# A hybrid decoder layer on one core: normal form in two fused operations, transposes and logits between the halves of the output projection, and routing of the first six tiles ahead of the last

## The reference

```python
def layer_norm(x, g, b):
    mu = jnp.mean(x, axis=-1, keepdims=True)
    var = jnp.mean(jnp.square(x - mu), axis=-1, keepdims=True)
    return (x - mu) * lax.rsqrt(var + LN_EPS) * g + b

mix = jnp.concatenate([y_conv, y_sb, y_gla], axis=-1) @ w_out
x = layer_norm(ALPHA * x + mix, ln1_g, ln1_b)                      # called x1 below

scores = jax.nn.sigmoid(x @ router_w)                              # (T, 16)
sel = scores + router_bias
grp = sel.reshape(T, 4, 4)
grp_score = jnp.sum(lax.top_k(grp, 2)[0], axis=-1)                 # sum of the two best of a group
_, top_group = lax.top_k(grp_score, 1)                             # the best group
_, top_idx = lax.top_k(where(expert in top_group, sel, -inf), 2)   # its two best experts
gate = scores of the two, divided by their sum
for e in range(16):
    y = y + gate[:, e:e+1] * ((silu(t @ w1[e]) * (t @ w3[e])) @ w2[e])
x = layer_norm(ALPHA * x + y, ln2_g, ln2_b)
```

## Time and profile before

| what | value |
|---|---|
| median of 3 runs | 959.66 us |
| the profiled execution: its own time | 959.35 us |
| its span on the core | 957.7 us |
| PE busy | 907.1 us (95%) |
| DVE busy | 630.0 us (66%) |
| ACT busy | 482.1 us (50%) |
| POOL busy | 281.8 us (29%) |
| granted clock of PE, mean | 0.984 |

### The profile page before, as it was taken

The page is one execution under the profiler, slowest core; times in us unless marked ns, Lnnn a source line. Parts: engine busy times, 40 slices in busy tenths (PEclk is TensorE's granted clock), DMA queues, the critical chain, the costliest instruction groups (busy, mean ns, idle before and its releaser), DMA issues.

```text
span 957.7 us, 16841 instructions
## 1 busy us (share of the span) xinstructions
PE 907.1 (95%) x6272; PEld 704.8 (74%) x6272; DVE 630.0 (66%) x833; ACT 482.1 (50%) x756; POOL 281.8 (29%) x250
## 2 busy tenths in 40 slices
PE   9999999999999999979999989999999999999970
PEld 7788999897777777758888667677777777777750
DVE  4211732666564665686655898888888888888785
ACT  3221532225564464662222616666666666666683
POOL 3000000000000000022000078666666666666334
PEclk9999999999999999999999999999999999999995
DMA  9301111001010030028632279999999999999973
GB/s 263 72 23 44 45 45 44 1 1 45 23 44 23 23 78 28 17 92 322 255 132 110 89 213 267 331 352 352 328 334 328 334 335 326 323 321 330 341 268 149
DMA packets 102140, 168.90 MB, mean 176 GB/s; under 512 B 24949, under 2 KB 48685, under 8 KB 102080
## 3 DMA queue, kind: packets, MB, share of 16 engines
q1 hardware_dynamic: 88720, 143.74, 43.7%
q0 software_dynamic: 10320, 23.18, 10.1%
q10 hardware_dynamic: 3040, 1.19, 0.5%
HBM read 143.81 MB, written 24.54 MB: 176 GB/s over the span
## 4 chain that ended last, share of the span: by engine, by line
PE 85%; DVE 6%; ACT 3%; DMA 3%; issue 2%; POOL 1%; SPq 0%; POOLq 0%; DVEq 0%; ACTq 0%
PE bank L896 11%; PE bank L898 11%; PE bank L897 11%; PE pz L896 7%; PE pz L897 7%; PE pz L898 7%; PE pz L1252 5%; PE bank L1356 3%; PE pz L1012 3%; PE pz L1279 3%; PE bank L1350 3%; PE bank L1357 3%; PE bank L1090 3%; PE bank L1106 2%; POOL slot_tokens L688 1%
## 5 line engine op out<-in xcount | busy, mean ns | idle before, releaser
L2014 DVE TENSOR_TENSOR el<-er,eh 128x1024 fp32r<-128x1024 f32 x192 | 223.9, 1219 | 29.9 <-ACT eh L1603 29.8
L1603 ACT ACTIVATE eh<-er 128x1024 fp32r<-128x1024 f32 x192 | 189.8, 1050 | 7.7 <-PE pz L898 7.7
L635 POOL MEMSET rw<- 128x128 f32 x1 | 0.2, 207 | 415.1 <-DVE mix L1938 415.1
L1945 DVE TENSOR_TENSOR_SCAN Qs<-Qs,own 128x128 f32<-128x128 f32 (+7 forms) x48 | 65.0, 1354 | 69.7 <-ACT Qs L1490 69.7
L896 PE MATMUL bank<-xT_hi,w_hi 128*128 128x512 f32 (+1 forms) x264 | 106.1, 402 | 1.9 <-DVE xT_lo L1830 1.9
L896 PE MATMUL pz<-eh,xh 128*128 128x512 f32 x256 | 102.8, 402 | 1.1 <-DVE xl L2035 1.1
L898 PE MATMUL bank<-xT_hi,w_lo 128*128 128x512 f32 (+1 forms) x264 | 102.4, 388 | 0.0
L897 PE MATMUL bank<-xT_lo,w_hi 128*128 128x512 f32 (+1 forms) x264 | 101.9, 386 | 0.0
L897 PE MATMUL pz<-el,xh 128*128 128x512 f32 x256 | 99.9, 390 | 0.0
L898 PE MATMUL pz<-eh,xl 128*128 128x512 f32 x256 | 99.8, 390 | 0.0
L762 POOL DMA_INDIRECT xg<-x_scratch,tabQ x52 | 82.3, 1582 | 15.8 <-issue 15.8
(11 more groups left out here) (358 smaller groups left out, 1830.1 us busy)
## 6 DMA issues: line engine op xcount, KB each, us to landing
er<-in_w_dram SPq DMA_DIRECT2D x192, 512.0 KB, 7.6
w_raw<-in_w_in_dram SPq DMA_DIRECT2D x21, 512.0 KB, 3.8
x_row<-in_x_dram SPq DMA_DIRECT2D x8, 512.0 KB, 8.9
xres<-in_x_dram SPq DMA_DIRECT2D x8, 512.0 KB, 5.7
sum_scratch<-x SPq DMA_DIRECT2D x8, 512.0 KB, 4.0
x_scratch<-x1p SPq DMA_DIRECT2D x8, 512.0 KB, 2.6
cx<-sum_scratch SPq DMA_DIRECT2D x8, 512.0 KB, 7.6
out_dram<-cx SPq DMA_DIRECT2D x5, 512.0 KB, 3.0
```

Source lines behind the costliest of these rows:

```text
L1603: act.activation(eh[:, p, :], er[:, p, :], ACT.Copy).then_inc(S["eh_ok"], 1)
L1945: dve.tensor_tensor_scan(Qs[:, h, 0:W][:, ::-1], Qs[:, h, 0:W][:, ::-1], own1[:, T - W:][:, ::-1], 0.0, ALU.mult, ALU.max).then_inc(S["sca ...
L2014: dve.tensor_tensor(el[:, p, :], er[:, p, :], eh[:, p, :].bitcast(F32), ALU.subtract).then_inc(S["el_ok"], 1)
```

## The change

Four things change, and no amount of arithmetic in the large products.

1. *Normal form.* The three passes become two: (x1 - mean) * gain over 1024 columns as soon as the mean is there, and then that times the inverse deviation, plus shift, in two halves of 512 columns. Each half of the statistics is taken right behind its half of the residual.
2. *PE's order.* Tile i-1 is turned between the halves of tile i, and its logits stand in the middle of the second half; the sums of its groups follow the tile. So everything stands one tile behind instead of two. A turn waits for each half of x1 by itself.
3. *Routing in two parts.* Tiles 0 to 5 are routed (`route_mask(0)`) by DVE ahead of the residual of tile 7; PE counts their slots before it turns tile 7. Tiles 6 and 7 are the second part. The slots are summed in another bank (`posb` in `pp[0]`), and expert 0's keys are made in two parts (`first_keys`).
4. *Ranks.* Instead of ten operations one comparison of all 16 pairs, a product with a triangle, a difference with the transposed pairs, and one sum. POOL writes the triangle (`rlow`) and two small rows (`rtop`), with four instructions more.

The copy of the slots and the low part of expert 0's first weight piece (`piece_lo(0, 0)`) now stand behind the first gather's row numbers. In ACT's order the block copy of tile 7 (`x1_blocked`) stands ahead of its logits' copy, and the exp of the first part ahead of the turned tile 6.

```diff
@@ PE @@
+            def turn_x1(c):
+                if c >= 1:
+                    pe.wait_ge(S["x1t_ev"], c)
+                for half in range(2):
+                    pe.wait_ge(S["x1_ok"], 3 * c + 2 + half)
+                    for k in range(4 * half, 4 * half + 4):
                         last = pe.transpose(pz[1][:, k * P:(k + 1) * P], x1[:, c % 2, k * P:(k + 1) * P], ident[:, :])
                     last.then_inc(S["x1t_ps"], 1)
...
+                out_half(i, 0, range(NK))
+                turn_x1(i - 1)
+                if i >= 2:
+                    pe.wait_ge(S["res_ok"], 2 * (i - 2) + 2)
+                out_half(i, 1, range(NK // 2))
...
+                for half in range(2):
+                    logits(i - 1, half)
+                out_half(i, 1, range(NK // 2, NK))
+                sum_groups(i - 1)
...
+            positions(0)
+            spin(13, pp[1][:, 0:GLA_W])
+            turn_x1(NT - 1)
+            logits(NT - 1, 0)
+            logits(NT - 1, 1)
+            spin(3, pp[1][:, 0:GLA_W])
             sum_groups(NT - 1)
...
+            first_tokens(0)
+            spin(9)
+            pe.wait_ge(S["mask_ok"], 2)
+            positions(1)
+            spin(4)
+            first_tokens(1)
@@ ACT @@
+            piece_hi(0, 2)
+            act.wait_ge(S["lgm_ps"], NT - 1)
+            x1_turned(NT - 1, [(0, NK // 2, 1), (NK // 2, NK, 2)])
+            x1_blocked(NT - 1)
             groups_out(NT - 1)
-            exps(NT - 1, NT)
-            x1_blocked(NT - 1)
+            exps(1)
@@ DVE @@
+                link(dve.tensor_tensor(rge[:, groups, :, :], rows.unsqueeze(2).to_broadcast([P, m, EPG, EPG]),
+                                       rows.unsqueeze(3).to_broadcast([P, m, EPG, EPG]), ALU.is_ge))
+                link(dve.tensor_tensor(rge[:, groups, :, :], rge[:, groups, :, :],
+                                       rlow[:, :, :].unsqueeze(1).to_broadcast([P, m, EPG, EPG]), ALU.mult))
+                link(dve.tensor_tensor(rdif[:, groups, :, :], rge[:, groups, :, :], rge[:, groups, :, :].rearrange("p n a b -> p n b a"),
+                                       ALU.subtract))
+                link(dve.tensor_reduce(rord[:, t0:t1, :, :].rearrange("p i g j -> p (i g) j"), rdif[:, groups, :, :], AX.X, ALU.add))
...
+                if i == NT - 1:
+                    dve.wait_ge(S["gsum_ok"], 6 + 2 + EPG - 1)
+                    dve.wait_ge(S["tokc_ok"], 13 + NQ)
+                    route_mask(0)
...
+            first_keys(0)
+            dve.wait_ge(S["mixl_ok"], NT)
+            dve.tensor_copy(idb[:, :, :], idf[:, :, :]).then_inc(S["idb_ok"], 1)
+            route_gates(0)
+            route_mask(1)
+            route_gates(1)
```

More of the change, by code:

```diff
@@ L315, in build @@
         rnp = small("rnp", [P, 1])
+        assert place[0] <= M + 6 * K
+        place[0] = M + 14 * K
+        rgk = small("rgk", [P, NT, NGRP])
+        rek = small("rek", [P, NT, NGRP, EPG])
+        rge = small("rge", [P, NT * (NGRP + 1), EPG, EPG])
+        rdif = small("rdif", [P, NT * (NGRP + 1), EPG, EPG])
+        assert place[0] <= M + 20 * K
         oneh = rt("oneh", 24 * K, [P, 2, NT, TW], BF16)
@@ L1138, in _, with logits @@
                         last = pe.transpose(pz[1][:, k * P:(k + 1) * P], x1[:, c % 2, k * P:(k + 1) * P], ident[:, :])
                     last.then_inc(S["x1t_ps"], 1)
[L1140 to L1154, removed]
-                    for k in range(NK) if i == 0 else ():
+            def logits(c, half):
+                pe.wait_ge(S["x1t_ev"], c + 1 + (half if c == NT - 1 else 0))
+                for k in range(4 * half, 4 * half + 4):
+                    g = k % 4
+                    last = pe.matmul(po[TR * g:TR * g + TR, 0:P], rw[:, k, :], x1T[:, k, :], start=(k < 4), stop=(k >= NK - 4),
+                                     skip_group_check=True)
+                if half:
+                    last.then_inc(S["lgm_ps"], 1)
@@ new lines, in out_half @@
+            def out_half(i, half, ks):
+                ns = slice(half * 512, half * 512 + 512)
+                last = mm3(pe, ob[i % 2][half], 0, NK - 1, lambda k: (mixh[:, i % 2, k, :], mixl[:, i % 2, k, :]),
+                           lambda k: (wo_hi[:, k, ns], wo_lo[:, k, ns]), ks)
+                if ks[-1] == NK - 1:
+                    last.then_inc(S["ob_ps"], 1)
+            for i in range(NT):
+                pe.wait_ge(S["mixl_ok"], i + 1)
+                if i == 0:
+                    for k in range(NK):
@@ new lines, in whole_tokens, with first_tokens @@
+            def whole_tokens(b, t0, t1):
+                for i in range(t0, t1):
+                    last = pe.matmul(sids_bank[b][0][:, 0:2], oneh[:, b % 2, i, 0:P], idb[:, :, i], start=(i == 0), stop=(i == NT - 1),
+                                     skip_group_check=True)
+                if t1 == NT:
+                    last.then_inc(S["sids_ps"], 1)
+            def first_tokens(part):
+                t0, t1 = ROUTE_PARTS[part]
+                pe.wait_ge(S["oneh_ok"], 2 * part + 1)
+                spare_tokens(0, t0, t1)
+                pe.wait_ge(S["oneh_ok"], 2 * part + 2)
+                whole_tokens(0, t0, t1)
```

311 lines of the change are left out of this document (150 added, 161 removed).

## The result

The changed kernel takes 965.49 us (median of four runs, 963.98 to 966.67) against 959.68 us (959.18 to 961.2) on the same chip: ratio 1.0064, with a 95% interval of [1.0051, 1.0077]. It is 5.8 us slower, and the forecast of 960.2 us, with its range up to 963.0 us, was too low. The profiled execution took 963.98 us with a span of 961.9 us; before it was 959.35 and 957.7.

A forecast was written before the change was run, and what follows sets the result against it. PE bounds up to T, then a DVE-led chain, then PE again. T moves 3.3 + 2.4 = 5.7 us later, the chain shortens by 5.2: + 0.5 us, so 960.2 us, range 956.8 to 963.0.

The forecast's parts named there:

- What bounds the kernel: Whole kernel: PE up to 526.53, a chain DVE leads up to 556.45, then PE again, shifting as a whole.
- PE up to T: Up to the end of tile 7's products (T, 526.56 before): extra turns, logits, sums, borders cost 3.3 us (bounds 2.3, 4.0).
- Stall in tile 1: PE waits in tile 1 for x1 of tile 0: 2.4 us, all on the path (bounds 1.2 and 3.5).
- The clock behind it: PE's clock behind the stall of tile 1: the forecast let it stay full, with no lost time.
- The rival: Clock falls in tile 1 behind the new stall: 1.6 us of lost products, 961.8 us; chance 0.27.
- The case I had for it staying: Around 415.9 in the profile before, PE was busy 3.07 of 6.10 us and the clock stayed at 1.00.
- The case for falling: Near the start, after PE stood still for 1.90 us, the granted clock around it was 0.74 on average.
- Routing ahead of tile 7: DVE's routing of tiles 0 to 5 takes about 5.7 us, hidden with 1.2 us to spare.
- the third rival: First routing late for tile 7, as multi-dimensional, repeated operands run slower: 963.3 us at 1.5 times 5.7 us; chance 0.09.
- From T to expert 1's keys: Chain behind tile 7's products: mask at T + 11.2, firstQ at T + 13.5, expert 1's keys at T + 16.3, before T + 21.5.
- From there to xl: From expert 1's keys to the low part of expert 0's rows: as before, 8.35 us, ending at T + 24.7.
- one of my own signs of being wrong: Signs: T within 3 us of old, DVE idle between mask and expert 0, or over a microsecond's difference behind first product.

The follow-up runs named there:

- e2: Changed kernel with only tile 0's turn moved later in tile 1, its logits behind the half, its sum in tile 2; ratio to kernel before 1.0027.
- e15: Changed kernel with tile 0's turn late alone, the same edit as e2 in a later series; ratio to kernel before 1.0024.
- e9: The kernel before, unedited, run again on another chip for its profile; 958.76 us, ratio 0.9997.
- e11: Changed kernel with the sixteen scatters of slot_tokens held back until ScalarE has written silB of expert 0; ratio to kernel before 1.0075.
- e1: Changed kernel with 17 more dummy matmuls ahead of the first turn of x1 in tile 1; ratio to kernel before 1.0037.
- e3: Changed kernel with longer dummy runs in the routing (13 to 21, 9 to 20, 8 new); ratio to kernel before 1.0054.
- e16: Changed kernel with the longer dummy runs in the routing alone, as e3, in a later series; ratio to kernel before 1.0054.
- e17: e13 once more, unedited, on another chip: old order of turns with new routing and normal form; 956.36 us, ratio to kernel before 0.9962.
- e10: Changed kernel with tile 0's turn late, last exponential ahead of the row copy, longer dummy runs in the routing; ratio to kernel before 0.9997.
- e18: Kernel before with the fused normal form and 4 instead of 9 dummy matmuls ahead of the last turn; ratio to kernel before 0.9977.
- series 1, 2 and 4: Runs e1 to e4, e5 to e8 and e13 to e16; the kernel before took 973.4, 968.2 and 973.0 us in them.
- e4: Kernel before with the normal form in two fused operations alone; ratio to kernel before 1.0003.
- e5: The changed kernel itself, unedited, on another chip; ratio to kernel before 1.0093.
- e6: Changed kernel with tile 6's turn, logits and group sum behind the last products, 8 dummies instead of 13; ratio to kernel before 1.0124.
- e8: Changed kernel with the logits behind half 1 instead of in its middle; one run of 982.29 us.
- e14: The changed kernel, unedited, on the chip of its series; ratio to kernel before 1.0068.
- e7: Changed kernel with tile 0's turn late, tile 6's turn and logits behind the last products, last exponential earlier, longer dummy runs; ratio to kernel before 1.0010.
- e13: Changed kernel with the old order of turns, logits and sums, tiles 0 to 4 routed early, exponential and xl earlier, longer dummies; ratio to kernel before 0.9915.

## Why the prediction was wrong

**What bounds the kernel: right.** PE up to T, the chain that DVE leads, and a shift as a whole behind the first product (- 0.2 us).

**PE up to T: 3.3 forecast, 4.15 measured**, outside my bound of 4.0. I priced the blocks from a cluster and gave 0.1 us a tile for borders; each block that interrupts the products pays for its own restart, 0.23 us a tile.

**Stall in tile 1: 2.4 forecast, 3.35 measured**, of which 2.87 us are idle time. The load landed at 443.61 instead of 443.08, and PE began tile 1 at 440.25 instead of 440.63. It was shown to be of the turn's place by e2 and e15, where nearly all of it is gone.

**The clock behind it: the step that failed.** I let the clock stay, at no cost, and gave its fall 0.27 at 1.6 us; it fell and cost 1.6 us. The rival's price was right, its chance too low. The case I had for it staying was a stretch with 3 us of idle time at full clock, in which PE's work was light. The case for falling had dense products behind the gap, as here. The trace before held a nearer one that I didn't read: a gap of 2.71 us ahead of tile 0's own products, at 428.20, and 3.4 us of half clock behind it. e9 shows that this gap isn't always followed by a fall, and nor is the stall near the start (1.00 over 29 to 38 us in e9 and in the profile after), so it didn't make the fall certain, but it was a reason for more than 0.27. The Trainium skill (TensorE: Matmul & The Clock Gate, the table of why this matters) asks only that gaps longer than this one be avoided; here one of 2.87 us was enough, and one of 2.23 us in e11, and the measurement decides. e1 shows the cause: with dummies in the gap the products behind it run 0.23 us apart.

**Routing ahead of tile 7: right.** 6.1 us instead of 5.7, hidden. The difference with its transposed second operand took 1.02 us for 480 elements where its neighbours took 0.66: the price of the third rival's mechanism, too small to make it decide.

**From T to expert 1's keys: right in every step**, with the fused pass at 1.28 us for my 1.24. The Trainium skill (VectorE: DVE Perf Modes, the perf-mode tier table) gives fp32 operations with two tensor sources half the rate of those with one, and the trace agrees: 1.28 us against 0.81.

**From there to xl: 8.35 forecast, 9.2 measured.** The fused and early routing leaves PE idle for 1.50 and 1.92 us with short matmuls between. The clock fell a second time, and PE, which I had taken to be off the path there, came late with expert 1's slots and the turned rows: DVE stood idle between the mask and expert 0, one of my own signs of being wrong. e3 and e16 put the clock's share at 0.4 us; the other 0.4 us stay with the clock at 1.00; 0.36 of them are DVE's idle time ahead of `spm`, and what it waits for the profile doesn't show ("issue"). I looked for a new wait on DVE and not at what a shorter chain does to PE's clock. The tail gave 4.4 us instead of 5.2.

Together, from the forecast + 0.5 us: 0.5 + 0.85 (blocks) + 0.95 (stall) + 1.6 (clock) + 0.85 (tail) - 0.4 (tile 1 began earlier) = 4.35 us, and the first product came 4.38 us later. The - 0.4 is chance on both sides: tile 0 began 1.18 us earlier in the profile after (427.02), the profiled execution of the kernel before lost some 0.9 us to half clock ahead of tile 1, and the one after waited there 1.51 us for `wo_lo` (at 438.32), which no other trace has. The profiled execution took 4.6 us more, 0.4 of them outside its span. The other three runs took 1.3 to 2.7 us more than it, where I had added 0.3 us for the median, with mean clocks of 0.976 to 0.978 against 0.980; they have no timeline, so where they lost more is open. My range treated the clock, the stall and the borders as alternatives, but they lie one behind the other on the same engine and add: with the clock's 1.6 us alone the forecast would have been 961.8, inside the range.

## What to carry to other kernels

Work moved ahead into a saturated engine costs its full length plus a restart of the stream at each cut. Before moving it, ask whether the engine behind needs it early: here the routing gained nearly the same with the old order (first at T + 26.8 in e17, T + 26.1 in e10), and the faster normal form alone was worth 2 us with fewer dummy matmuls in front of the turn (e18). Where a wait is added in a dense stream of products, price the half clock behind it as the likely case, even if another execution of the same kernel shows none, and put the consumer where its input is already there. A shorter chain around an idle TensorE has to be priced with its clock as well.

## What the runs showed of the hardware

On the two chips of series 1, 2 and 4 every kernel took longer: the kernel before by 8.5 to 13.7 us (968.2 to 973.4 against 959.7), the others by similar amounts. The traces place it between 555 and 615 us: from ACT's silA of expert 1 (590.27 in the kernel before) to the end all twenty take 366.8 to 369.0 us. The kernel before has no trace on these chips; e4, which differs from it by the normal form alone, takes 413.6 us from its first product to the end, where the kernel before took 399.9 on the first chip. In e5 ACT's xh starts 5.2 us behind its data and PE shows gaps put down to issue; from 565 to 575 almost nothing is moved (1 GB/s):

```profile
564.01 0.42 PE L1293 MATMUL pz<-er,xB 128*32 128x256 f32 x2 [1.01 <-issue]
565.52 1.08 ACT L1710 ACTIVATE xh<-bank 128x512 fp32r<-128x512 f32 x2 [14.11 <-remote]
...
565.00:575.00 10.00, 7.12 (x15) 3.91 (x15) 8.61 (x17) 2.37 (x3) 6.50 (x7) 0.56 0.02 1
```

In the same kernel on the first chip xh followed its data by 0.1 us. In the series on these chips the first product came at T + 31 to 34 in e1, e2, e5, e6, e8, e14 and e15, all with the clock fallen in the routing, and at T + 26.5 to 28 in e3, e7, e13 and e16, which had longer dummy runs (in e13 the clock still fell, from 539 to 543). e4, with the long dummy runs of the kernel before, had T + 31.0 where that has T + 31.25. Whether the clock is the cause or only goes with it, and what holds the engines up, wasn't settled.

PE's clock also fell after short idle times: 3.4 us at half clock behind a gap of 2.87 us in dense products, 10.2 us after gaps of 1.50 and 1.92 us among short ones, and about 3 us in e10 after none above 0.6 us. It isn't the same in each execution: the gap of 2.7 us ahead of tile 0 was followed by half clock in eleven of twenty traces.
